# A top-2 mixture of experts on one core: where the token rows of a group of 32 slots come from

## The reference, cut to what matters

```
combine = zeros over 16 experts, two of them set per token      # top-1 group of 4, then top-2 inside it
for e in range(16):
    a, b = split(t @ w_up[e], 2)                                # 1024 -> 2 x 512
    y += combine[:, e:e+1] * ((silu(a) * b) @ w_down[e])        # 512 -> 1024
```

## Time and profile before

| | us |
|---|---|
| three timed runs | 1289.64, 1292.05, 1292.47 (median 1292.05) |
| the profiled execution | 1286.74, of which the profile's span is 1284.9 |
| TensorE busy (matmul) | 1191.6, 93% of the span |
| VectorE, ScalarE, GpSimd busy | 525.7, 310.7, 166.7 |
| mean granted TensorE clock | 0.965 |
| weights moved by SyncE's queue | 298.43 MB in all |

### The profile page before, as it was taken

One profiled execution on the slowest core, in us unless ns is written; L12 is line 12 of the kernel. 1 busy time (PEld: TensorE's weight loads), 2 busy tenths in 40 slices (PEclk: granted clock), 3 DMA queues, 4 the chain that ended last, 5 costly groups with the idle time before them and its releaser, 6 DMA issues.

```text
span 1284.9 us, 29972 instructions
## 1 busy us (share of the span) xinstructions
PE 1191.6 (93%) x12606; PEld 708.2 (55%) x12606; DVE 525.7 (41%) x1322; ACT 310.7 (24%) x637; POOL 166.7 (13%) x203
## 2 busy tenths in 40 slices
PE   4999999999999999999986999999999999999993
PEld 1455555556555565555554555466555565666551
DVE  2522223355553444343435200175663434444445
ACT  4111111200232222222223000154232222222223
POOL 0300000031001111111110100045001111111112
PEclk8799999999989999999997999989989999999997
DMA  9928878870259989245399632433055899999402
GB/s 326 392 102 288 301 268 299 299 295 8 92 230 389 409 323 410 79 166 196 120 408 391 212 105 91 149 106 98 2 185 192 344 368 409 381 409 409 186 0 82
DMA packets 104651, 305.80 MB, mean 238 GB/s; under 512 B 7136, under 2 KB 11424, under 8 KB 104256
## 3 DMA queue, kind: packets, MB, share of 16 engines
q1 hardware_dynamic: 98800, 298.43, 61.1%
q0 software_dynamic: 1648, 5.20, 1.4%
q10 hardware_dynamic: 4128, 1.05, 0.3%
HBM read 302.05 MB, written 2.62 MB: 237 GB/s over the span
## 4 chain that ended last, share of the span: by engine, by line
issue 45%; PE 42%; POOL 5%; DVE 4%; ACT 2%; DMA 1%; POOLq 0%; SPq 0%; ACTq 0%; DVEq 0%
PE bank L596 40%; POOL yg L551 4%; POOL P L569 1%; PE bank L1008 1%; DMA ring<-in_w_ada 1%; ACT x L1134 1%; DVE P L1681 1%; DVE st L1633 1%; PE bank L761 0%; PE bank L642 0%; POOLq L548 0%; DVE x L1452 0%; ACT tok L1119 0%; ACT arow L1051 0%; DVE hT L1463 0%
## 5 line engine op out<-in xcount | busy, mean ns | idle before, releaser
L596 PE MATMUL bank<-ring,xgT 128*32 128x256 f32 x4224 | 242.6, 381 | 13.9 <-issue 7.9
L596 PE MATMUL bank<-hT,ring 128*128 128x384 f32 x640 | 208.0, 487 | 0.1
L596 PEld LDWEIGHTS bank<-ring,xgT 128*32 128x32 f32 x4224 | 145.9, 110 | 93.5 <-issue 14.9
L596 PEld LDWEIGHTS bank<-hT,ring 128*128 128x128 f32 x640 | 121.1, 190 | 83.7 <-issue 0.8
L551 POOL TENSOR_TENSOR yg<-ysb,gate_s 128x256 f32<-128x256 f32 x132 | 93.9, 733 | 559.9 <-ACT ysb L1191 559.9
L596 PE MATMUL bank<-ring,heT 128*32 128x256 f32 x2112 | 127.6, 382 | 13.1 <-DVE heT L1615 10.6
L1613 DVE TENSOR_TENSOR he<-sa,bank 128x128 f32<-128x128 f32 x66 | 18.9, 287 | 221.5 <-ACT sa L1188 221.5
L596 PE MATMUL bank<-yg,ohT 32*128 32x256 f32 x1632 | 107.3, 391 | 1.5 <-POOL yg L551 1.5
L596 PE MATMUL bank<-tok,hot 128*32 128x256 f32 x1680 | 103.6, 379 | 0.0
L596 PEld LDWEIGHTS bank<-ring,heT 128*32 128x32 f32 x2112 | 62.2, 109 | 62.5 <-DVE heT L1615 25.8
L596 PEld LDWEIGHTS bank<-yg,ohT 32*128 32x128 f32 x1632 | 74.6, 184 | 34.4 <-issue 27.3
(11 more groups left out here) (230 smaller groups left out, 1316.3 us busy)
## 6 DMA issues: line engine op xcount, KB each, us to landing
ring<-in_moe_w_up SPq DMA_DIRECT2D x64, 2048.0 KB, 14.2
ring<-in_moe_w_down SPq DMA_DIRECT2D x32, 2048.0 KB, 19.3
ring<-in_w_ada SPq DMA_DIRECT2D x24, 2048.0 KB, 16.3
ring<-in_hy_w_in SPq DMA_DIRECT2D x6, 2048.0 KB, 16.3
ring<-in_na_w_qkv SPq DMA_DIRECT2D x6, 2048.0 KB, 20.7
ring<-in_hy_w_out SPq DMA_DIRECT2D x2, 2048.0 KB, 14.4
ring<-in_na_w_out SPq DMA_DIRECT2D x2, 2048.0 KB, 7.8
bm<-in_na_bias SPq DMA_DIRECT2D x16, 256.0 KB, 3.2
```

Source lines behind the costliest of these rows:

```text
L596: return nc.tensor.matmul(out, lhsT, rhs, start=first, stop=last)
```

## The change

At dispatch the slots are cast to integers (`idx_i`), and GpSimd writes the rows of the 384 tokens into a DRAM list `slots` at their two slots each, with six indirect DMAs of 128 rows of 4 KB (one for each of two choices and three tiles of tokens). The list was cleared before from a constant of zeros, layer 0's after the filter stage and layer 1's at the start of attention. ScalarE then loads a group's 32 rows from the list straight into `xgs`, in the layout of four column blocks, once TensorE has turned the rows before. Only the first group of a layer is still gathered with one-hot matmuls. `one_hot` for later groups, its `rel`, and ScalarE's copies of gathered rows are gone. The transposes of `xgs` now write bank 0, and `he`'s transpose and the down-projection write bank 1.

```diff
+        slots = [nc.dram_tensor(f"slots{l}", [(MAX_BLOCKS + 2) * SLOT_TOK, D], f32).ap() for l in range(DEPTH)]
...
+            def clear_slots(l):
+                pool.dma_start(slots[l].rearrange("(a p) d -> p a d", p=SLOT_TOK),
+                               A["k_zero"].unsqueeze(1).to_broadcast([SLOT_TOK, MAX_BLOCKS + 2, D])).then_inc(slots_cleared[l], 16)
+
+            clear_slots(0)
...
+                for t in range(TT):
+                    for h in range(2):
+                        wait_evacuated(pool, G_AT[f"tok{l}_{t}"] + h)
+                pool.wait_ge(slots_cleared[l], 16)
+                pool.wait_ge(S["idx_i_ready"], 1)
+                for k in range(2):
+                    for t in range(TT):
+                        nc.gpsimd.indirect_dma_start(
+                            out=slots[l][:, :], out_offset=bass.IndirectOffsetOnAxis(ap=idx_i[:, k, t:t + 1], axis=0),
+                            in_=tok[:, t, :], in_offset=None).then_inc(S["slots_filled"], 16)
...
                     with pe.Fori(0, nb) as b:
                         w1 = base + b + 1
-                        pe.wait_ge(S["ysb_ready"], w1 - 1)
+                        pe.wait_ge(S["xgT_ready"], w1)
...
-                        nc.tensor.transpose(ps[0][:, 256:384], he[:], ident[:]).then_inc(S["he_turned"], 1)
-                        pe.wait_ge(S["xgs_ready"], w1 + 1)
+                        nc.tensor.transpose(ps[1][:, 256:384], he[:], ident[:]).then_inc(S["he_turned"], 1)
+                        pe.wait_ge(S["xgs_in"], w1 * 16)
                         turn_gathered()
...
-                                last = mm(ps[0][32 * o:32 * o + 32, 0:256], heT[:, 32 * q:32 * q + 32],
+                                last = mm(ps[1][32 * o:32 * o + 32, 0:256], heT[:, 32 * q:32 * q + 32],
                                           wd[:, q, 256 * o:256 * o + 256], q == 0, q == 3)
                         last.then_inc(S["y_ready"], 1)
-                        pe.wait_ge(S["xgT_ready"], w1 + 1)
-                        pe.wait_ge(S["oh_ready"], w1 + 2)
-                        gather()
...
+                def group_rows(at_, turned):
+
+                    act.wait_ge(S["xg_turned"], turned)
+                    act.dma_start(xgs[:], slots[l][bass.ds(at_, SLOT_TOK), :].rearrange("s (j c) -> j s c", j=4)).then_inc(S["xgs_in"], 16)
+
                 act.wait_ge(nb_ready, l + 1)
                 total = act.value_load(NBi[0:1, 32:33], min_val=EXPERTS, max_val=MAX_BLOCKS)
+                act.wait_ge(S["slots_filled"], 96)
+                group_rows(SLOT_TOK, 1)
                 with act.Fori(0, total) as g:
                     act.wait_ge(S["up_ready"], g + 1)
                     nc.scalar.activation(sa[:], ps[0][:, 0:128], ACT.Silu).then_inc(S["sa_ready"], 1)
+                    group_rows(g * SLOT_TOK + 2 * SLOT_TOK, g + 2)
                     act.wait_ge(S["y_ready"], g + 1)
                     act.wait_ge(S["yg_ready"], g * 2 + 2)
-                    nc.scalar.activation(ysb[:], ps[0][:, 0:256], ACT.Copy).then_inc(S["ysb_ready"], 1)
-                    gathered(g + 3)
+                    nc.scalar.activation(ysb[:], ps[1][:, 0:256], ACT.Copy).then_inc(S["ysb_ready"], 1)
...
-                def one_hot(n):
...
+                v.tensor_copy(idx_i[:], idxf[:]).then_inc(S["idx_i_ready"], 1)
...
                 with dve.Fori(0, total) as g:
-                    one_hot(g + 2)
                     dve.wait_ge(S["sa_ready"], g + 1)
```

More of the change, by code:

```diff
@@ L156, in shape_constants @@
     moe[:, MC_ROW] = np.arange(128) % SLOT_TOK
-    return {"k_dft": dft, "k_moe": moe}, feat, cols
+    return {"k_dft": dft, "k_moe": moe, "k_zero": np.zeros((SLOT_TOK, D), np.float32)}, feat, cols
 def side_by_side(A, feat, cols):
@@ L273, in build @@
         pos = at("pos", [128, TT, 16], RM + 4160)
+        idx_i = at("idx_i", [128, 2, TT], RM + 4128, i32)
         wk = at("wk", [128, 2, TT], RM + 4352)
@@ L348, in build @@
             moe_sems.append({n: sem(f"{n}{l}") for n in (
-                "oh_pair", "oh_moved", "oh_ready", "gathered", "xgs_ready", "xg_turned", "xgT_ready", "up_ready", "sa_ready",
+                "oh_pair", "oh_ready", "gathered", "xgs_ready", "idx_i_ready", "slots_filled", "xgs_in", "xg_turned", "xgT_ready", "up_ready", "sa_ready",
                 "he_ready", "he_turned", "heT_ready", "y_ready", "ysb_ready", "yg_ready", "ohk_ready", "ohT_ready", "srow_ready", "combined")})
+        slots_cleared = [sem(f"slots_cleared{l}") for l in range(DEPTH)]
+        slots = [nc.dram_tensor(f"slots{l}", [(MAX_BLOCKS + 2) * SLOT_TOK, D], f32).ap() for l in range(DEPTH)]
         block = ctx.enter_context(nc.Block())
@@ L543, in moe_side @@
                 nc.gpsimd.memset(ohT[:], 0.0).then_inc(S["ohT_ready"], 1)
+                for t in range(TT):
[8 more added lines that the diff above has]
+                            in_=tok[:, t, :], in_offset=None).then_inc(S["slots_filled"], 16)
                 pool.wait_ge(nb_ready, l + 1)
-                pool.wait_ge(evacuated[G_AT[f"gf{l}"] % 8], G_AT[f"gf{l}"] // 8 + 1)
+                wait_evacuated(pool, G_AT[f"gf{l}"])
                 total = pool.value_load(NBi[0:1, 32:33], min_val=EXPERTS, max_val=MAX_BLOCKS)
@@ L563, in _ @@
             nc.gpsimd.memset(bm[:, :, :, SAMPLE:], 0.0).then_inc(pad_ready, 1)
+            clear_slots(1)
             for u in range(TT * PAIRS):
@@ L842, in gather, with turn_gathered @@
                     last.then_inc(S["gathered"], 1)
-                def turn_gathered(b=1):
+                def turn_gathered():
                     for c in range(2):
-                        last = nc.tensor.transpose(ps[b][:, 256 + 128 * c:384 + 128 * c], xgs[:, 128 * c:128 * c + 128], ident[:])
+                        last = nc.tensor.transpose(ps[0][:, 256 + 128 * c:384 + 128 * c], xgs[:, 128 * c:128 * c + 128], ident[:])
                     last.then_inc(S["xg_turned"], 1)
@@ L897, in expert @@
                             for o in range(4):
-                                last = mm(ps[0][32 * o:32 * o + 32, 0:256], heT[:, 32 * q:32 * q + 32],
+                                last = mm(ps[1][32 * o:32 * o + 32, 0:256], heT[:, 32 * q:32 * q + 32],
                                           wd[:, q, 256 * o:256 * o + 256], q == 0, q == 3)
                         last.then_inc(S["y_ready"], 1)
-                        pe.wait_ge(S["xgT_ready"], w1 + 1)
-                        pe.wait_ge(S["oh_ready"], w1 + 2)
-                        gather()
-                    pe.wait_ge(S["ysb_ready"], base + nb)
+                    pe.wait_ge(S["xgT_ready"], base + nb + 1)
                     mm(ps[0][0:2, 0:2], ident[:, 0:2], ident[:, 0:2]).then_inc(expert_done[l], 1)
@@ L919, in moe @@
                 pe.wait_ge(S["xgs_ready"], 1)
-                turn_gathered(0)
-                pe.wait_ge(S["oh_ready"], 2)
-                gather()
+                turn_gathered()
                 pe.wait_ge(spread_evac, 4 * l + 4)
@@ L927, in moe @@
                 pe.wait_ge(S["ohT_ready"], 1)
-                pe.wait_ge(S["xgT_ready"], 1)
                 for e in range(EXPERTS):
@@ L934, in moe @@
                 pe.wait_ge(S["yg_ready"], total * 2 + 2)
+                pe.wait_ge(S["xgs_in"], total * 16 + 16)
                 combine(total * 2 + 1, True).then_inc(acc_ready, 1)
-                pe.wait_ge(S["xgs_ready"], total + 2)
             project_out(0, yT)
@@ L1175, in moe @@
                     nc.scalar.activation(wk_all[:, k, :], ps[6 + k][:, 0:TOK], ACT.Copy).then_inc(spread_evac, 1)
[L1176 to L1180, removed]
+                act.wait_ge(S["gathered"], 1)
+                nc.scalar.activation(xgs[:], ps[1][:, 0:256], ACT.Copy).then_inc(S["xgs_ready"], 1)
                 act.wait_ge(spread_ready, 2 * l + 2)
                 nc.scalar.activation(pos_all[:, 1, :], ps[7][:, 0:TOK], ACT.Copy).then_inc(spread_evac, 1)
-                gathered(2)
+                def group_rows(at_, turned):
+                    act.wait_ge(S["xg_turned"], turned)
+                    act.dma_start(xgs[:], slots[l][bass.ds(at_, SLOT_TOK), :].rearrange("s (j c) -> j s c", j=4)).then_inc(S["xgs_in"], 16)
                 act.wait_ge(nb_ready, l + 1)
                 total = act.value_load(NBi[0:1, 32:33], min_val=EXPERTS, max_val=MAX_BLOCKS)
+                act.wait_ge(S["slots_filled"], 96)
+                group_rows(SLOT_TOK, 1)
                 with act.Fori(0, total) as g:
@@ L1574, in moe @@
                 dve.wait_ge(idx_ready, l + 1)
-                def one_hot(n):
[L1578 to L1591, removed]
+                v.tensor_tensor(oh2[:].rearrange("p k t s -> p (k t) s"),
+                                mc[:, MC_IOTA:MC_IOTA + SLOT_TOK].unsqueeze(1).to_broadcast([128, 2 * TT, SLOT_TOK]),
+                                idxf[:].rearrange("p k t -> p (k t)").unsqueeze(2).to_broadcast([128, 2 * TT, SLOT_TOK]), ALU.is_equal
```

(10 more changed lines are left out.)

## The result

The kernel after takes 1413.76 us (median of 4 runs, 1409.19 to 1415.44) against 1290.85 us before on the same chip. The ratio is 1.094, with a 95% interval of 1.0919 to 1.0961. The profiled execution took 1414.45 us, its span 1412.6. The forecast of 1342 us had the sign right, but the loss is about 2.5 times as large as it said, and outside the range.

The account below looks back on a forecast made before the run. TensorE was taken to bound the kernel, the weight stream close behind. Per layer 222 + 100 + 7 = 329 us, two layers 658 - 607 = +51 us, 1286.74 to 1338; 5.3 us more for timed runs gave 1342, range 1250 to 1375.

Parts of the forecast that it names:

- The gather's 1.30 us: Expert loop: the gather leaves TensorE in all 66 groups, 86 us; a group could run in 7.53 us, not 8.83.
- The clears: Clearing the lists, 5.5 MB read and written each: first costs nothing, second at start of attention 0 to 13 us, taken 0.
- L: Landing time of a group's row load: 10.3 us while weights stream, 2.9 otherwise; the change breaks even at 8.6.
- What a group gets instead: Expert loop: ScalarE's 128 KB load into the single buffer xgs, landing 10.3 us beside weights, closed cycle 10.8 us.
- the prediction's own sum: One layer's expert stage: 222 us streaming, 100 us for 13.3 free groups, 7 us expert changes, 329 us in all.
- Rival 1: Row load on four of 16 engines, 32 rows each: landing 11.1 us, layer 346 us, total 1377 us; chance 0.27.
- two signs: Row load landing over 11 us, and weight pieces landing later than their 14.2 us.
- the 20 that the prediction named and did not count: TensorE's clock granted 0.92 instead of 1.00 because of waits: 8% of 7.5 us for 40 groups, 20 us.
- Beginning of a layer: Six scatters beside expert 2's weights land at about 386, delaying group 0's SiLU and group 1's rows: 8 to 15 us, taken 13.
- Rival 3: Start of a layer: scatters cost 5 us each, 15 to 20 us more a layer, steady state free, about 1290; chance 0.05.
- The load at the end of a layer: End of a layer's expert loop: the extra row load has landed before the last combine.
- Rival 2: Row load spread over all 16 engines, 8 rows each: landing 6.3 us, layer about 285 us, 1255 us; chance 0.28.

Follow-up runs that it names:

- e4: Kernel before, all but the first two groups' gathers left out, one small matmul standing in for the 24: 1263.6 us, ratio 0.9782, with 65 groups.
- e1: Kernel after, each load's 128 rows taken in DRAM order so they lie on all 16 engines, the copy to xgT restoring order: 1273.4 us, ratio 0.9862.
- e9: Kernel after, each group's one load replaced by four, one per column block, order of rows in DRAM unchanged: 1289.8 us, ratio 0.9998.
- e8: Kernel after, list loads replaced by a one-column copy of xgs on ScalarE, no wait for the list: 1231.9 us, ratio 0.9529, with 65 groups.
- e7: Kernel after with the edits of e1 and e6 together: 1261.7 us, ratio 0.976.
- e6: Kernel after, SyncE made to wait for the six scatters before loading expert 2's weights: 1410.0 us, ratio 1.0899.

## Why the prediction was right or wrong

**What held.** The gather's 1.30 us do go: a free group has a period of 7.56 us (1067.89 to 1075.45), forecast 7.53. The cycle is closed over one buffer. The clears cost nothing that shows: TensorE has no wait for either, layer 0's stage begins 1.6 us later than before and in e4, which clears nothing, 2.2 later. The sign follows from L > 8.6, and L was 12.0. e1 and e9 lie on the other side of that point with L of 5.9 and 6.8, and neither is slower than before.

**The step that failed: "What a group gets instead", L = 10.3 us.** The value was the difference between two transfers of 128 rows per engine, added to the landing of bias loads that lie on all engines. It priced "beside the stream" as one sum, without asking how many rows each engine gets. The runs put three terms in its place: 3.9 us to the first row (1.35 without the stream), 7.3 us for 32 rows on each of four engines (2.0 without the stream), and 0.75 from the last row to the landing. L is 12.0 and the cycle 12.8, where the forecast had 10.3 and 10.8. That is 22 us a layer in the prediction's own sum, 44 of the 77 us that it was short; the rest is below.

**Rival 1 was the mechanism.** Its terms were 6.4 us of turns and 4.7 for the rest; measured are 7.3 and 4.7. It gave L = 11.1 and missed by 0.9 us. Of its two signs, L over 11 came clearly and later weight pieces only just (14.7 us for the up-projection's, 14.2 before). The forecast held that nothing in the trace showed a transfer on fewer engines, which was true, and took the nearest row over the form of the source; that made it the likelier case. The rule of the Trainium skill that stood beside it ("DMA: Bandwidth & Descriptors", the section named above) was the better guide, and the packets of queue 10 bear it out.

**Rival 1's sum was still 15 us a layer short** (346, measured 361). L was 0.9 us short, and three terms were missing. The cycle holds 0.6 to 0.9 us beside L, not 0.5. The start costs 15.5 us and not 13. The clock falls in the waits: after 31 of the 33 waits of the turn the down-projection takes 2.8 to 3.6 us and not 1.93, and its matmuls take 485 ns on average, in e8, without these waits, 382. Where the next turn waits too, that is hidden, as the cycle goes by the load. It shows in the nine groups that follow a wait (the starts left out) and don't wait themselves: 8.9 to 10.4 us from turn to turn and not 7.54, at most 17 us together, near the 20 that the prediction named and did not count. With a cycle of 12.8 and a start of 23 us the prediction's own sum gives 23 + 199 + 16.5 x 7.53 + 7 = 353 us a layer. The last 8 may be those nine groups for the most part (an estimate; no run changes the clock alone).

**Beginning of a layer.** The form of it was right: the six scatters beside expert 2's weights, ScalarE in front of the SiLU. The list was full at 394 and not 386: 3.1 MB in 24 us are 131 GB/s, a third of 410 and not half. Group 0's SiLU came 17 us later and not 7. Issuing the scatters takes 0.95 to 1.26 us each on GpSimd, near the 0.9 taken. Rival 3, 5 us of POOL for each, is out.

**The load at the end of a layer** was said to have landed ahead of the last combine, and was put at nothing. In layer 0 it had not. No group uses its rows, but the combine waits for it, and it is issued beside the QKV weights. The load as it stands in the chain that ended last, and TensorE's instructions around it in order of time:

```profile
737.06 9.86 DMA xgs<-slots
```

```profile
738.80 0.19 PE L616 MATMUL bank<-first 128*2 128x2 f32 x2
746.96 2.94 PE L616 MATMUL bank<-yg,ohT 32*128 32x256 f32 x24 [7.97 <-DMA xgs<-slots]
```

Before, this combine began 1.0 us after the end of the last expert and took 1.58 us; now it is 8.2 and 2.94 (the granted clock is 0.50 in it). That is 8.6 of the 9.0 us between the stages. In e8, which has no such load, the stretch is 283.8 us against 278.3 before: 1.3 us more ahead of the combine, 1.3 in it, and 3 us further on that stay open. e1, e7 and e9 have 282.3 to 284.6 us, e4 279.3.

**Rival 2** had the right steps for a load on 16 engines (L 6.3, measured 5.9 in e1; the bound moves to the weights), and 1255 us for it; e1 gives 1273. Its missing part is the start, 24 us to the end of expert 0; with that shortened, e7 gives 1262.

## What to carry to other kernels

Before a small load goes beside a stream, count the engines it lies on, from the slowest dimension of both of its sides, and the rows on each: here every row beside the stream waited for about one row of it, whatever its own bytes. Where the load is in a loop over one buffer, that landing time is the loop's period, so price it beside the stream and not from a quiet stretch. A sequencing edit that releases a small load and a large one by the same event can give its gain to the large one, as in e6. A load whose data nobody reads still costs its landing time where something waits for its semaphore.

An extra matmul in a loop may be the cover of a wait; taking it out alone brought 0.5 of its 1.3 us here. Two row buffers, with the load issued a group ahead, were not tried.

## What the runs showed of the hardware

- A row's turn beside a stream of 4 KB rows costs 0.23 us for 1 KB and 0.17 us for 32 bytes; without the stream 32 rows of 1 KB on an engine take 2.0 us in all.
- The time from issue to the first row rises by 2.5 us beside another queue's stream: from 1.35 to 3.9 on four engines, from 0.97 to 3.5 on sixteen.
- The issue itself takes ScalarE's queue 0.54 us on four engines and 0.34 on sixteen.
- An indirect scatter of 128 rows of 4 KB lands in 4.0 us (median) alone and in 13.3 beside the stream.
